# HGRN2 recurrence: the input gate's multiply moved into the exponents, and two VectorE steps reordered

## The chip, the cores and the metric

One core of one Trainium2 chip runs the whole program. The metric is the device time of one execution in microseconds.

## The reference, cut to what matters

The program is one inference step of a two-layer decoder trunk for a prompt of 512 tokens and 8 sample streams of 4 tokens each (544 columns in all), model width 1024, all in fp32. Layer 0 mixes with a gated convolution and windowed attention, layer 1 with an HGRN2 recurrence of 8 heads; each layer ends in a convolutional feed-forward part. The change is in layer 1's recurrence. Per head, with 128 key and 128 value channels:

```python
q, f, i, g = jnp.split(xn @ w_in, ...)
log_f = jnp.logaddexp(jnp.log(lb), jnp.log1p(-lb) + jax.nn.log_sigmoid(f))
k_in = (1.0 - lb) * jax.nn.sigmoid(-f)
# in chunks, with G the running sum of log_f inside a chunk:
decay = jnp.exp(jnp.where(causal, G_t - G_s, -jnp.inf))
A = einsum(q_t, k_s, decay)                       # scores inside the chunk
o = A @ v + (q * exp(G)) @ S
S = exp(G_last) * S + (k * exp(G_last - G)).T @ v
# then
o = rms_norm(o, norm_g) * silu(g);  out = o @ w_out
```

## The kernel before, in words

Every projection is a run of weight "units" (128 output channels). A unit is two halves of four 128-row weight tiles. ScalarE rounds each half to fp32r (`w_hi`, L844), VectorE takes the rest (`w_lo`, L1299), and TensorE makes three passes of 2 matmuls for each tile (`half`, L428): 24 matmuls a half. Halves follow each other all through the program. A weight half is split four halves ahead of its use.

The recurrence is written by hand between these halves. A head has 4 units (forget logit f, q, v, gate g), so 8 halves, and after each half every engine runs one "tick" (`hgrn_tick(t, prev, cur)`, t = 0 to 7): part of the current head `cur` and part of the one before, `prev`, whose outputs are still being finished. Each engine runs its own list strictly in order, and the engines meet at semaphores. Heads 1 to 7 have `prev`; head 0 has none, and only its last two units lie inside the ticks. After head 7, ticks 0 to 4 for `prev` = 7 run between the first halves of the output projection. In what follows head n is the stretch in which `cur` = n.

What the engines do in a head, as far as the change or the prediction's steps touch it:

- Tick 1. VectorE evacuates the forget logit (`head_out`, L1722) and clamps it (L1725). ScalarE makes exp(-f), ln(1 + .), exp(-.) = sigmoid(f) (L1198 to L1202), copies two score levels into `AT` (L1209, L1213) and rounds a weight half. TensorE multiplies score levels 1 and 2 (L704, L709).
- Tick 2. VectorE takes score levels (L1709), makes `kk` = the input gate k (L1782, one fused instruction on exp(-f), 1 - lb and sigmoid(f)) and the forget gate (L1783, L1785); ScalarE takes its logarithm (L1219); VectorE's scan gives `G` (L1790).
- Tick 3. VectorE evacuates q, splits a weight half, then runs `kd_and_diag`: `kd` = G_last - G (L1671, L1673 for the sample columns) and `E2` = G - G of the middle of each 8 columns (L1676, L1678). After that it adds the new sample state `Snew` (L1773, two instructions). TensorE runs the output matmuls (L748 to L762). ScalarE makes exp(kd), and GpSimd multiplies it by `kk` (L1950).
- Tick 4. TensorE waits for `Snew` (it needs the two PSUM banks) and for ScalarE's squares, then sums squares (L769, L770). VectorE scales the output gate (L1752, L1754) and makes the differences of levels 0 and 1 (`level_ops`, L1646, one 128x512 instruction a level). ScalarE makes `E1` = exp(diff) (L1236) and `E2` = exp(-diff) (L1237).
- Tick 5. VectorE evacuates v, splits a weight half, makes the head's output product (L1759), the level 2 difference, the transposed keys' rest (L1684), `y_lo` (L1764), the q half of level 0 (`level_q`, L1652), and `E2` times `kk` (L1803). ScalarE rounds `y_hi` (L1232). GpSimd makes `E1` times q (L1956), then `key_level` for level 0 (L1969), `qG` = exp(G) times q (L1963), then `key_level` for levels 1 to 3. TensorE transposes `kd` (L779; in head 0 at tick 6).
- Tick 6. TensorE transposes v (L786). VectorE makes the level 3 difference.
- Tick 7. ScalarE makes the level 3 exponentials (L1242, L1243), then scales the old sample states (L1251, eight instructions).
- Tick 0 of the next head. ScalarE rounds a weight half (L844) and starts the output gate. VectorE splits the half (L1299), takes the diagonal scores (L1709, L1739) and chains the states (L1657, L1660). TensorE multiplies the diagonal (L718 on `c_E`), and later, in tick 2, levels 3 and 4 (L718 on `lev`).

The lines that set who waits are these two of TensorE, with the order of VectorE in tick 3:

```python
if t == 4: pe.wait_ge(C["snew_ready"], 2 * prev + 2)
if t == 3: kd_and_diag(cur); dve.wait_ge(C["s0_scaled"], prev + 1); ... Snew += A[z]
```

## Time and profile before

| what | value |
|---|---|
| median of 3 runs | 1373.17 us (1372.12 to 1373.91) |
| the profiled execution's own time | 1372.79 us |
| its span, first to last instruction | 1371.0 us |
| mean granted TensorE clock | 0.992 |
| TensorE matmuls busy | 1331.7 us, 97% |
| VectorE busy | 820.6 us, 60% |
| ScalarE busy | 590.2 us, 43% |
| GpSimd busy | 249.5 us, 18% |
| recurrence with its ticks | 631 to 916 us of the span |
| one head of the steady part (761.08 to 795.20) | PE 33.01, DVE 28.11, ACT 22.66, POOL 9.53 us busy of 34.12 |

The span is what the trace covers; the time of the execution is 1.79 us longer, since it holds the start and the end around it. "Busy" counts an instruction from its start to its end, and an instruction that stands waiting for something inside itself counts as busy. The idle time in brackets at a row's end is the engine's pause before that row, with what ended it.

### The profile page before, as it was taken

Reading aid. Unit: us, or ns where it says so; the run is one execution under the profiler, and the core shown is the slowest. Engines: PE = TensorE matmul, PEld = TensorE weight load, DVE = VectorE, ACT = ScalarE, POOL = GpSimd, SP = SyncE. Lnnn points to the kernel's source line nnn. Section 1 sums busy time; section 2 is a strip of 40 time slices with the busy share of each in tenths; the row PEclk is TensorE's granted clock in tenths of the full one; section 3 lists DMA queues with packets and bytes.
Section 4 is the critical chain, followed back from the end, with each engine's and each line's share of the span. In section 5 each row is a group of like instructions: output and inputs, shape, how many; then the busy total and the mean of one; then the engine's idle time right before and its main releaser. Section 6 shows DMA issues by size and latency. Waiting matters only on the chain.

```text
span 1371.0 us, 30087 instructions
## 1 busy us (share of the span) xinstructions
PE 1331.7 (97%) x11724; PEld 1297.3 (95%) x11724; DVE 820.6 (60%) x1401; ACT 590.2 (43%) x1198; POOL 249.5 (18%) x373
## 2 busy tenths in 40 slices
PE   8999999999999999997999999989999999999997
PEld 8988999999999999996999999989999999999996
DVE  6467486656555632248788888867665555562224
ACT  5344354433333322236666666655533333332221
POOL 2123121111111101001222222212111111120000
PEclk9999999999999999999999999999999999999999
DMA  7411231222222322212222222323122232232211
GB/s 272 122 49 47 78 109 47 93 81 87 91 78 91 120 86 86 89 51 91 96 94 94 94 94 94 95 79 96 57 94 78 91 92 92 82 125 95 85 43 66
DMA packets 39682, 123.37 MB, mean 90 GB/s; under 512 B 4232, under 2 KB 12040, under 8 KB 39496
## 3 DMA queue, kind: packets, MB, share of 16 engines
q1 hardware_dynamic: 35400, 111.92, 25.1%
q10 hardware_dynamic: 4048, 10.20, 2.2%
q8 instruction: 41, 0.67, 0.2%
q0 software_dynamic: 176, 0.44, 0.1%
q14 instruction: 17, 0.14, 0.0%
HBM read 113.98 MB, written 8.57 MB: 89 GB/s over the span
## 4 chain that ended last, share of the span: by engine, by line
PE 77%; DVE 11%; ACT 6%; issue 5%; POOL 1%; DMA 0%; ACTq 0%; DVEq 0%; SPq 0%; POOLq 0%
PE acc L428 73%; DVE w_lo L1299 1%; ACT w_hi L844 1%; DVE lev L1646 1%; DVE x L1501 1%; ACT Snew L1251 1%; DVE Snew L1773 1%; DVE mix L1496 1%; DVE AT L1709 1%; PE aux L585 1%; DVE scratch L1759 1%; ACT AT L1213 0%; DVE h_lo L1308 0%; PE aux L597 0%; DVE lev L1652 0%
## 5 line engine op out<-in xcount | busy, mean ns | idle before, releaser
L1299 DVE TENSOR_TENSOR w_lo<-raw,w_hi 128x512 fp32r<-128x512 f32 (+1 forms) x372 | 316.3, 854 | 342.5 <-ACT w_hi L844 342.0
L428 PE MATMUL acc<-h_hi,w_hi 128*128 128x272 f32 x2208 | 478.7, 295 | 7.0 <-DVE h_lo L1308 2.4
L428 PE MATMUL acc<-h_hi,w_lo 128*128 128x272 f32 x2208 | 466.0, 289 | 0.0
L428 PE MATMUL acc<-h_lo,w_hi 128*128 128x272 f32 x2208 | 465.1, 289 | 0.0
L428 PEld LDWEIGHTS acc<-h_hi,w_hi 128*128 128x128 f32 x2208 | 351.6, 189 | 19.3 <-issue 8.0
L844 ACT CAST w_hi<-raw 128x512 fp32r<-128x512 f32 (+1 forms) x372 | 236.5, 642 | 288.2 <-PE acc L428 283.2
L428 PEld LDWEIGHTS acc<-h_lo,w_hi 128*128 128x128 f32 x2208 | 352.0, 190 | 0.2
L428 PEld LDWEIGHTS acc<-h_hi,w_lo 128*128 128x128 f32 x2208 | 349.6, 190 | 0.0
L428 PE MATMUL acc<-g_hi,w_hi 128*128 128x272 f32 x704 | 153.1, 288 | 0.0
L428 PE MATMUL acc<-g_hi,w_lo 128*128 128x272 f32 x704 | 153.0, 289 | 0.0
L428 PE MATMUL acc<-g_lo,w_hi 128*128 128x272 f32 x704 | 152.3, 288 | 0.0
L428 PEld LDWEIGHTS acc<-g_hi,w_hi 128*128 128x128 f32 x704 | 113.4, 188 | 0.1
L428 PEld LDWEIGHTS acc<-g_lo,w_hi 128*128 128x128 f32 x704 | 113.4, 189 | 0.1
L428 PEld LDWEIGHTS acc<-g_hi,w_lo 128*128 128x128 f32 x704 | 112.7, 189 | 0.0
L1924 POOL TENSOR_TENSOR scratch<-scratch,rstd 128x544 f32<-128x544 f32 x44 | 59.9, 1361 | 169.3 <-ACT scratch L1127 169.3
L1127 ACT ACTIVATE scratch<-scratch 128x544 f32<-128x544 f32 x44 | 29.0, 659 | 112.2 <-DVE scratch L1321 112.2
L1859 POOL TENSOR_TENSOR scratch<-scratch 128x272 f32<-128x272 f32 (+1 forms) x35 | 39.1, 1116 | 199.1 <-ACT scratch L994 151.3
L428 PE MATMUL acc<-y_hi,w_hi 128*128 128x272 f32 x256 | 69.6, 292 | 1.7 <-DVE y_lo L1764 1.6
L1133 ACT CAST g_hi<-scratch 128x544 f32 (+1 forms) x44 | 28.5, 647 | 98.1 <-DVE scratch L1605 93.6
L428 PE MATMUL acc<-y_hi,w_lo 128*128 128x272 f32 x256 | 68.8, 289 | 0.0
L428 PE MATMUL acc<-y_lo,w_hi 128*128 128x272 f32 x256 | 68.3, 287 | 0.0
L1123 ACT ACTIVATE scratch<-scratch,vec 128x544 f32<-128x544 f32 x44 | 33.0, 751 | 65.7 <-DVE scratch L1599 64.0
(247 smaller groups left out, 1424.4 us busy)
## 6 DMA issues: line engine op xcount, KB each, us to landing
raw<-in_w_up SPq DMA_DIRECT2D x88, 512.0 KB, 3.5
raw<-in_w_down SPq DMA_DIRECT2D x32, 704.0 KB, 4.1
raw<-in_w_in_c SPq DMA_DIRECT2D x32, 512.0 KB, 3.5
raw<-in_w_in_ab SPq DMA_DIRECT2D x18, 512.0 KB, 3.7
raw<-in_w_out_ab SPq DMA_DIRECT2D x8, 512.0 KB, 3.6
S<-in_state ACTq DMA_DIRECT2D x8, 512.0 KB, 3.6
o_ss<-Snew ACTq DMA_DIRECT2D x8, 512.0 KB, 2.7
raw<-in_w_out_c SPq DMA_DIRECT2D x8, 512.0 KB, 3.6
```

The costliest lines, as they stand in the source:

```text
L428: mm = pe.matmul(acc[out][:, t, 0:H], w[slot][:, wc], mv[:, kk_, t * H:(t + 1) * H], start=start and k == 0 and q == 0, stop=stop and k == ...
L585: mm = pe.matmul(A[g][:, j * 256 + lo_k:j * 256 + 256], q_sb[rows, 2 * pair + j, n * WIN:(n + 1) * WIN], k_sb[rows, (n - 1) * WIN + lo_k:( ...
L844: act.copy(w_hi[slot][:, to:to + kts * P], raw[n % 4][:, cols]).then_inc(hi_ready, 1)
L1123: act.activation(S[1][:], S[0][:], ACT.Copy, scale=vec[:, bass.ds(w + u + 2 * i, 1)]).then_inc(tap_ready, 1)
L1127: act.activation(S[2][:], S[1][:], ACT.Gelu_apprx_tanh).then_inc(act_done, 1)
L1133: act.copy(g_hi[:, u + 2 * i, :], S[3][:]).then_inc(g_hi_ready, 1)
L1251: i_ = act.activation(Snew[:, b, :], S0[:, b, :], ACT.Copy, scale=eG[:, last:last + 1])
L1299: dve.tensor_tensor(w_lo[slot][:, to], raw[n % 4][:, cols], w_hi[slot][:, to], ALU.subtract).then_inc(lo_ready, 1)
L1496: step.mark(dve.tensor_tensor(mix[:, k, cols(t)], mix[:, k, cols(t)], S[3][:, cols(t)], ALU.mult))
L1501: dve.scalar_tensor_tensor(x[:, k, cols(t)], mix[:, k, cols(t)], col(gain, k), x[:, k, cols(t)], ALU.mult, ALU.add).then_inc(x_new, 1)
L1859: pool.tensor_tensor(S[2][:, q], S[2][:, q], S[k % 2][:, q], ALU.add).then_inc(sq_added, 1)
L1924: pool.tensor_tensor(S[2][:], S[2][:], rstd[:], ALU.mult).then_inc(gate_ready, 1)
```

## The change

The key-side products of k with an exponential become sums before the exponential. Since k = (1 - lb) exp(-f) sigmoid(f), ln k = ln(1 - lb) - f + ln sigmoid(f). VectorE's fused instruction of tick 2 now makes -ln k in `S[0]` in place of `kk`, from the logit, ln(1 - lb) and ln(1 + exp(-f)). The buffer of `kk` is named `Gk`. It holds the sigmoid and the forget gate first, and after the scan `Gk` = G - ln k, a new 128x544 addition. The differences that need k use `Gk` where they used `G`. GpSimd's multiplies of `kd` and of the four levels are gone, VectorE's of `E2` too. `E1` needs a difference of its own, so the diagonal has four VectorE instructions in place of two, and a level's difference is two instructions of 128x256 in place of one of 128x512. `kd_and_diag` is cut in two; the diagonal's part stands behind the sample state. GpSimd starts on `E1` when ScalarE's first exponential of the pair is done. ln(1 - lb) is made once, after layer 0's mixer, by one VectorE and one ScalarE instruction of 8 columns. VectorE waits for GpSimd's `qG` of the head before it overwrites q.

```diff
@@ TensorE, hgrn_tick
-                        pe.wait_ge(C["diag_ready"], 2 * prev + 2)
+                        pe.wait_ge(C["diag_ready"], prev + 1)
+                        pe.wait_ge(C["diag_exp"], 2 * prev + 2)
...
-                        pe.wait_ge(C["lev_ready"], 8 * prev + 8)
+                        pe.wait_ge(C["lev_ready"], 4 * prev + 4)
@@ ScalarE, after_out and hgrn_tick
+                if post == 1:
+                    act.wait_ge(C["lb_ready"], 2)
+                    act.activation(lb[:, 4, :], lb[:, 3, :], ACT.Ln).then_inc(C["lb_done"], 1)
...
-                        step.mark(act.activation(S[0][:], S[0][:], ACT.Exp, scale=-1.0))
+                        step.mark(act.activation(S[1][:], S[0][:], ACT.Exp, scale=-1.0))
...
-                        act.activation(S[1][:], S[1][:], ACT.Exp, scale=-1.0).then_inc(C["sig_ready"], 1)
+                        act.activation(Gk[:], S[1][:], ACT.Exp, scale=-1.0).then_inc(C["sig_ready"], 1)
...
-                        act.activation(kd[:], kd[:], ACT.Exp).then_inc(C["kd_exp"], 1)
+                        act.activation(kd[:], kd[:], ACT.Exp).then_inc(C["kd_ready"], 1)
...
-                        act.activation(E1[:], E2[:], ACT.Exp)
+                        act.activation(E1[:], E1[:], ACT.Exp).then_inc(C["diag_exp"], 1)
                         act.activation(E2[:], E2[:], ACT.Exp, scale=-1.0).then_inc(C["diag_exp"], 1)
@@ VectorE, level_ops
-                dve.tensor_tensor(v, g, mid, ALU.subtract).then_inc(C["lev_diff"], 1)
+                dve.tensor_tensor(v[:, :, 0, :], gk[:, :, 0, :], mid, ALU.subtract)
+                dve.tensor_tensor(v[:, :, 1, :], g[:, :, 1, :], mid, ALU.subtract).then_inc(C["lev_diff"], 1)
@@ VectorE, kd_and_diag becomes kd_ops and diag_ops
+                step.mark(dve.tensor_tensor(Gk[:], G[:], S[0][:], ALU.add))
+                step.wait(dve)
...
+            def diag_ops(cur):
...
+                for to, of in ((E1, G), (E2, Gk)):
+                    dve.tensor_tensor(to[:, 0:TP].rearrange("p (c s) -> p c s", s=8),
+                                      of[:, 0:TP].rearrange("p (c s) -> p c s", s=8),
+                                      g8[:, :, 3:4].broadcast_to([P, TP // 8, 8]), ALU.subtract)
@@ VectorE, hgrn_tick and head_out
+                    if t == 3:
+                        dve.wait_ge(C["qG_ready"], cur)
...
-                        kd_and_diag(cur)
+                        kd_ops(cur)
                     dve.wait_ge(C["s0_scaled"], prev + 1)
...
+                    if cur is not None:
+                        diag_ops(cur)
...
-                    dve.scalar_tensor_tensor(kk[:], S[0][:], one_lb, S[1][:], ALU.mult, ALU.mult)
+                    dve.scalar_tensor_tensor(S[0][:], S[0][:], ln_one_lb, S[1][:], ALU.subtract, ALU.add)
...
-                    dve.wait_ge(C["diag_exp"], cur + 1)
-                    dve.tensor_tensor(E2[:], E2[:], kk[:], ALU.mult).then_inc(C["diag_ready"], 1)
@@ GpSimd, hgrn
-                    pool.wait_ge(C["kd_exp"], cur + 1)
-                    pool.tensor_tensor(kd[:], kd[:], kk[:], ALU.mult).then_inc(C["kd_ready"], 1)
...
-                    pool.wait_ge(C["diag_exp"], cur + 1)
+                    pool.wait_ge(C["diag_exp"], 2 * cur + 1)
                     pool.tensor_tensor(E1[:], E1[:], qn[:], ALU.mult).then_inc(C["diag_ready"], 1)
-                    for l in range(4):
-                        key_level(l, cur)
...
+                    pool.tensor_tensor(qG[:], eG[:], qn[:], ALU.mult).then_inc(C["qG_ready"], 1)
```

VectorE, the loop over heads 1 to 6, from the end of tick 3's weight split through tick 4 (`c_G`, `c_Gk`, `c_E`, `c_kd` are G, Gk, E1 or E2, kd), before:

```order
L1299 TENSOR_TENSOR w_lo<-raw,w_hi 128x512
L1671 TENSOR_TENSOR c_kd<-c_G 128x512
L1673 TENSOR_TENSOR c_kd<-c_G 128x32
L1676 TENSOR_TENSOR c_E<-c_G 128x512
L1678 TENSOR_TENSOR c_E<-c_G 128x32
...
L1773 TENSOR_TENSOR Snew<-Snew,aux 128x512
...
L1299 TENSOR_TENSOR w_lo<-raw,w_hi 128x512
L1752 SCALAR_TENSOR_TENSOR c_sg<-aux,vec,c_sg 128x512
L1754 SCALAR_TENSOR_TENSOR c_sg<-aux,vec,c_sg 128x32
L1646 TENSOR_TENSOR lev<-c_G 128x512 x2
L1722 TENSOR_TENSOR c_vv<-acc,rstd 128x544
```

and after the change:

```order
L1303 TENSOR_TENSOR w_lo<-raw,w_hi 128x512
L1676 TENSOR_TENSOR c_Gk<-c_G,scratch 128x544
...
L1680 TENSOR_TENSOR c_kd<-c_G,c_Gk 128x512
L1682 TENSOR_TENSOR c_kd<-c_G,c_Gk 128x32
...
L1791 TENSOR_TENSOR Snew<-Snew,aux 128x512
L1690 TENSOR_TENSOR c_E<-c_G 128x512
L1693 TENSOR_TENSOR c_E<-c_G 128x32
L1690 TENSOR_TENSOR c_E<-c_Gk,c_G 128x512
L1693 TENSOR_TENSOR c_E<-c_Gk,c_G 128x32
```

Ahead of the state stand three instructions in place of four; the diagonal's four stand behind it, ahead of the weight split, the gate and four half-width level differences, all before the evacuation of v.

GpSimd, the same loop, ticks 3 to 7, before:

```order
L1950 TENSOR_TENSOR c_kd<-c_kd,c_kk 128x544
...
L1956 TENSOR_TENSOR c_E<-c_E,c_qn 128x544
...
L1969 TENSOR_TENSOR lev<-lev,c_kk 128x4x64
L1963 TENSOR_TENSOR c_qG<-c_eG,c_qn 128x544
...
L1969 TENSOR_TENSOR lev<-lev,c_kk 128x8x32
```

and after:

```order
L1975 TENSOR_TENSOR c_E<-c_E,c_qn 128x544
...
L1979 TENSOR_TENSOR c_qG<-c_eG,c_qn 128x544
```

The two products with q now stand next to each other, and nothing of `kd` or the levels is left on this engine.

## Rows read from the trace of the kernel before

**Rows 1.** Waits of TensorE, whole span: engine, line waited for, us in total, times, longest.
```profile
PE aux L769 <- DVE Snew L1773: 6.2, 7, 1.0
```

**Rows 2.** Timeline of TensorE, heads 1, 4, 5 and 7: start us, us, engine line op.
```profile
664.02 0.45 PE L704 MATMUL aux<-lev 128*64 128x64 f32 x8
...
678.50 0.73 PE L769 MATMUL aux<-scratch,ones 128*128 128x272 f32 x2 [0.44 <-DVE Snew L1773]
...
765.56 0.45 PE L704 MATMUL aux<-lev 128*64 128x64 f32 x8
...
780.96 0.73 PE L769 MATMUL aux<-scratch,ones 128*128 128x272 f32 x2 [0.97 <-DVE Snew L1773]
...
815.10 0.73 PE L769 MATMUL aux<-scratch,ones 128*128 128x272 f32 x2 [0.95 <-DVE Snew L1773]
...
883.48 0.72 PE L769 MATMUL aux<-scratch,ones 128*128 128x272 f32 x2 [0.98 <-DVE Snew L1773]
```

**Rows 3.** Timeline of VectorE, forget-logit evacuation to new sample state, heads 1 and 4.
```profile
664.13 0.72 DVE L1722 TENSOR_TENSOR scratch<-acc,rstd 128x544 f32<-128x544 f32 x1 [0.53 <-PE acc L428]
...
766.59 0.72 DVE L1722 TENSOR_TENSOR scratch<-acc,rstd 128x544 f32<-128x544 f32 x1
...
778.21 0.69 DVE L1671 TENSOR_TENSOR c_kd<-c_G 128x512 f32<-128x512 f32 x1
...
779.62 1.28 DVE L1773 TENSOR_TENSOR Snew<-Snew,aux 128x512 f32<-128x512 f32 x2
```

**Rows 4.** Timeline of VectorE, head 4, ticks 5 to 7 and the next tick 0.
```profile
785.18 0.72 DVE L1722 TENSOR_TENSOR c_vv<-acc,rstd 128x544 f32<-128x544 f32 x1 [1.50 <-PE acc L428]
...
787.36 1.26 DVE L1759 TENSOR_TENSOR scratch<-scratch,c_sg 128x544 f32<-128x544 f32 x1
788.54 1.84 DVE L1646 TENSOR_TENSOR lev<-c_G 128x512 f32<-128x512 f32 x1
...
792.38 0.71 DVE L1803 TENSOR_TENSOR c_E<-c_E,c_kk 128x544 f32<-128x544 f32 x1
...
796.70 0.75 DVE L1652 TENSOR_TENSOR lev<-lev,c_qn 128x256 f32<-128x256 f32 x2
797.94 0.69 DVE L1299 TENSOR_TENSOR w_lo<-raw,w_hi 128x512 fp32r<-128x512 f32 x1 [0.49 <-ACT w_hi L844]
```

**Rows 5.** Timeline of GpSimd, head 4, ticks 4 and 5.
```profile
785.52 1.36 POOL L1956 TENSOR_TENSOR c_E<-c_E,c_qn 128x544 f32<-128x544 f32 x1 [4.41 <-ACT c_E L1237]
...
788.00 1.84 POOL L1963 TENSOR_TENSOR c_qG<-c_eG,c_qn 128x544 f32<-128x544 f32 x1
```

**Rows 6.** Timeline of ScalarE, head 4, tick 5 to the next tick 0.
```profile
788.74 0.65 ACT L1232 CAST y_hi<-scratch 128x544 f32 x1 [1.22 <-DVE scratch L1759]
...
794.33 0.42 ACT L1242 ACTIVATE lev<-lev 128x256 f32<-128x256 f32 x1 [1.24 <-DVE lev L1646]
...
797.30 0.60 ACT L844 CAST w_hi<-raw 128x512 fp32r<-128x512 f32 x1
```

**Rows 7.** Timelines of GpSimd, VectorE and TensorE, head 0, ticks 4 to 6.
```profile
646.90 1.37 POOL L1956 TENSOR_TENSOR c_E<-c_E,c_qn 128x544 f32<-128x544 f32 x1 [0.37 <-ACT c_E L1237]
...
645.66 1.42 DVE L1299 TENSOR_TENSOR w_lo<-raw,w_hi 128x512 fp32r<-128x512 f32 x1 [0.53 <-ACT w_hi L844]
647.00 2.42 DVE L1646 TENSOR_TENSOR lev<-c_G 128x512 f32<-128x512 f32 x2
...
646.59 1.11 PE L779 MATMUL aux<-ident,c_kd 128*128 128x128 f32 x4 [4.25 <-POOL c_kd L1950]
...
650.11 1.12 PE L786 MATMUL aux<-ident,c_vv 128*128 128x128 f32 x4 [2.20 <-DVE c_vv L1722]
```

**Rows 8.** Busy time by stretch: us, PE, PEld, DVE, ACT, POOL, PEclk, DMA, GB/s.
```profile
654.00:656.00 2.00, 2.00 (x10) 2.00 (x10) 2.00 (x4) 0.81 (x4) 0.79 (x1) 0.50 0.07 23
```

**Rows 9.** Timeline of TensorE, last head's output part.
```profile
895.48 0.43 PE L718 MATMUL aux<-c_E 128*32 128x32 f32 x29 [0.73 <-issue]
...
905.39 0.70 PE L748 MATMUL aux<-vbd,kt_s 96*128 96x512 f32 x2 [0.25 <-DVE AT L1709]
```

More of the change, by code:

```diff
@@ L236, in build @@
                 with ExitStack() as b:
-                    kk, G, qn, vv, gn, sg, eG, kd, qG, E1, E2 = [
+                    Gk, G, qn, vv, gn, sg, eG, kd, qG, E1, E2 = [
                         sb(f"c_{n}", [P, T], F32, b)
-                        for n in ("kk", "G", "qn", "vv", "gn", "sg", "eG", "kd", "qG", "E1", "E2")]
+                        for n in ("Gk", "G", "qn", "vv", "gn", "sg", "eG", "kd", "qG", "E1", "E2")]
                     lev = [sb(f"lev{i}", [P, TP], F32, b) for i in range(len(SPANS))]
@@ L1641, in level_ops @@
             def level_ops(l, cur):
[L1643 to L1646 removed]
+                v, g, gk = [z.rearrange("p (n a s) -> p n a s", a=2, s=SPANS[l]) for z in (lev[l][:], G[:, 0:TP], Gk[:, 0:TP])]
+                mid = g[:, :, 0, SPANS[l] - 1:SPANS[l]].broadcast_to([P, TP // (2 * SPANS[l]), SPANS[l]])
+                dve.tensor_tensor(v[:, :, 0, :], gk[:, :, 0, :], mid, ALU.subtract)
+                dve.tensor_tensor(v[:, :, 1, :], g[:, :, 1, :], mid, ALU.subtract).then_inc(C["lev_diff"], 1)
             def level_q(l, cur):
@@ L1665, in states, with kd_ops @@
                 i_.then_inc(C["st_ready"], 1)
-            def kd_and_diag(cur):
+            def kd_ops(cur):
                 dve.wait_ge(C["G_ready"], cur + 1)
-                gp, gs_ = G[:, 0:TP].rearrange("p (c s) -> p c s", c=NCH), sample(G[:, TP:T])
+                step.mark(dve.tensor_tensor(Gk[:], G[:], S[0][:], ALU.add))
+                step.wait(dve)
+                gp, gk = [z[:, 0:TP].rearrange("p (c s) -> p c s", c=NCH) for z in (G, Gk)]
+                gs_, gks = sample(G[:, TP:T]), sample(Gk[:, TP:T])
                 dve.tensor_tensor(kd[:, 0:TP].rearrange("p (c s) -> p c s", c=NCH),
-                                  gp[:, :, CH - 1:CH].broadcast_to([P, NCH, CH]), gp, ALU.subtract)
-                dve.tensor_tensor(sample(kd[:, TP:T]), gs_[:, :, TS - 1:TS].broadcast_to([P, NB, TS]), gs_,
+                                  gp[:, :, CH - 1:CH].broadcast_to([P, NCH, CH]), gk, ALU.subtract)
+                dve.tensor_tensor(sample(kd[:, TP:T]), gs_[:, :, TS - 1:TS].broadcast_to([P, NB, TS]), gks,
                                   ALU.subtract).then_inc(C["kd_diff"], 1)
+            def diag_ops(cur):
+                gs_ = sample(G[:, TP:T])
                 g8 = G[:, 0:TP].rearrange("p (c s) -> p c s", s=8)
-                dve.tensor_tensor(E2[:, 0:TP].rearrange("p (c s) -> p c s", s=8), g8,
-                                  g8[:, :, 3:4].broadcast_to([P, TP // 8, 8]), ALU.subtract)
-                dve.tensor_tensor(sample(E2[:, TP:T]), gs_, gs_[:, :, 1:2].broadcast_to([P, NB, TS]),
-                                  ALU.subtract).then_inc(C["diag_diff"], 1)
+                for to, of in ((E1, G), (E2, Gk)):
+                    dve.tensor_tensor(to[:, 0:TP].rearrange("p (c s) -> p c s", s=8),
+                                      of[:, 0:TP].rearrange("p (c s) -> p c s", s=8),
+                                      g8[:, :, 3:4].broadcast_to([P, TP // 8, 8]), ALU.subtract)
+                    i_ = dve.tensor_tensor(sample(to[:, TP:T]), sample(of[:, TP:T]),
+                                           gs_[:, :, 1:2].broadcast_to([P, NB, TS]), ALU.subtract)
+                i_.then_inc(C["diag_diff"], 1)
             def kdT_lo(cur):
@@ L1791, in hgrn_tick @@
                 if prev is None and t == 3:
-                    kd_and_diag(cur)
+                    kd_ops(cur)
+                    diag_ops(cur)
                 if t == 4:
@@ L1948, in hgrn @@
                 if cur is not None:
-                    pool.wait_ge(C["kd_exp"], cur + 1)
-                    pool.tensor_tensor(kd[:], kd[:], kk[:], ALU.mult).then_inc(C["kd_ready"], 1)
-                if cur is not None:
                     if prev is None:
@@ L1954, in hgrn @@
                     pool.wait_ge(evac, tile("in_c", 1) + 4 * cur)
-                    pool.wait_ge(C["diag_exp"], cur + 1)
+                    pool.wait_ge(C["diag_exp"], 2 * cur + 1)
                     pool.tensor_tensor(E1[:], E1[:], qn[:], ALU.mult).then_inc(C["diag_ready"], 1)
-                    for l in range(4):
-                        key_level(l, cur)
-                        if l == 0:
-                            if prev is not None:
-                                pool.wait_ge(C["oc_done"], prev + 1)
-                            pool.wait_ge(C["eG_ready"], cur + 1)
-                            pool.tensor_tensor(qG[:], eG[:], qn[:], ALU.mult).then_inc(C["qG_ready"], 1)
-            def key_level(l, cur):
-                pool.wait_ge(C["lev_exp"], 4 * cur + l + 1)
-                v, k_ = [z.rearrange("p (n a s) -> p n a s", a=2, s=SPANS[l]) for z in (lev[l][:], kk[:, 0:TP])]
-                pool.tensor_tensor(v[:, :, 0, :], v[:, :, 0, :], k_[:, :, 0, :], ALU.mult).then_inc(C["lev_ready"], 1)
+                    if prev is not None:
+                        pool.wait_ge(C["oc_done"], prev + 1)
+                    pool.wait_ge(C["eG_ready"], cur + 1)
+                    pool.tensor_tensor(qG[:], eG[:], qn[:], ALU.mult).then_inc(C["qG_ready"], 1)
             pool.wait_ge(half_done, 2 * UNIT0["in_c"])
```

19 lines of the change are left out of this document (10 added, 9 removed).

## The prediction

> **What bounds the kernel now.** I read the page first: TensorE's matmuls are busy for 97% of the span. So I read next what TensorE waits for. The longest sum is 6.2 us in 7 waits for the new sample state, one per head from 1 to 7 [rows 1]. The timeline shows them: 0.44 us in head 1, then 0.95 to 0.98 us [rows 2]. From head 1 to head 7 the six steps take 883.48 - 678.50 = 204.98 us, 34.16 each; from head 4 to head 5 it is 34.14. A wait of 0.97 us can be short because TensorE is slow to ask, or because the state is late, so I followed it back with the chain of waits. VectorE takes the forget logit at 766.59 and TensorE goes on at 780.96, 14.37 us later; in head 1 it is 678.50 - 664.13 = 14.37 as well [rows 2, 3]. That piece is a fixed run of VectorE and ScalarE work. The start differs. In head 1 VectorE stood ready (idle 0.53 until TensorE's half was done) and started 0.11 us after TensorE went to the level matmuls (664.02). In head 4 TensorE was there at 765.56 and VectorE came only at 766.59, 0.92 us later than those 0.11 us allow [rows 2, 3]. It was still busy with tick 0, which had begun with a wait of 0.49 us for a weight half of ScalarE at 797.94 (the same point one head on) [rows 4]. ScalarE was late because it had waited 1.24 us for the level 3 difference at 794.33, and started that half at 797.30 [rows 6]. VectorE made that difference late because its tick 5 is stretched: the output product takes 1.26 us and the level 2 difference 1.84 us, while GpSimd multiplies [rows 4, 5]. So the steady heads are bound by a **loop of VectorE and ScalarE**: state, tick 5, level 3, sample scaling, weight half, states, logit, state. TensorE keeps up with 0.97 us to spare. What shortens the stretched tick 5 is worth time, up to the point where VectorE is ready when TensorE's half ends.
>
> **Piece 1, logit to sample state.** The evacuation of q, the scan and the split stay. Ahead of the state, two diagonal differences leave and the addition G - ln k comes. The four differences take 779.62 - 778.21 = 1.41 us [rows 3], a pair 0.70. The new addition is 128x544 from two SBUF operands, like the product at 792.38, 0.71 us [rows 4]; with the wait for its own result 0.74. Net +0.04 us. The fused instruction of tick 2 keeps its form. Putting the state ahead of the diagonal thus only pays for the addition. Piece 1 becomes 14.41 us.
>
> **Piece 2, state to the next logit.** I lay the changed lists on the times of head 4; the state's adds end at 780.9 [rows 3]. Then the diagonal, now four instructions: 1.41, to 782.3. Weight split 0.61 and the gate's two steps 0.8: 783.75. The differences of levels 0 and 1 are now four of 128x256. Two such instructions took 0.75 us from the first's start to the last's end [rows 4], 0.34 each when they follow one another; so 1.36, to 785.1. The evacuation of v started at 785.18 after 1.50 us of idle time [rows 4]. The 1.4 us of diagonal and 0.15 us for the split differences fit into this idle time, with nothing left over.
>
> GpSimd starts its product with q when the first exponential is done, one ScalarE instruction of 544 columns earlier than 785.52: `y_hi` has that size and takes 0.65 us, of which some 0.55 count in a row of them, so about 785.0 [rows 5, 6]. It and VectorE then want the same thing. When GpSimd's `qG` started at 788.00 VectorE's product of 1.26 us was still running to 788.62, and VectorE's level 2 difference started at 788.54 and ended at 790.38, 0.54 us after `qG` ended at 789.84 [rows 4, 5]. Undisturbed it is 0.68 us. This is what taking turns looks like, a whole instruction each, not a slowdown of both by a share. The **Trainium skill**, "SBUF — State Buffer", on who interferes with whom, states it as a rule: a VectorE instruction with two SBUF inputs and a GpSimd instruction hold a shared port pair in turn, and the loser blocks fully. The trace agrees in every such pair that I looked at; it matters most in head 0, below, where turns and shares give sums of their own.
>
> Taking turns: GpSimd's product runs 785.1 to 786.4, and `qG` follows at once to 787.7. VectorE's split, due at 786.53, waits for it and ends at 788.3; the output product runs free to 789.0, 0.4 us later than before. ScalarE's `y_hi` moves from 788.74 to 789.1. From there GpSimd is silent. Before, ScalarE took 797.30 - 788.74 = 8.56 us to its weight half, 1.24 of it waiting for level 3 [rows 6]. Now VectorE has level 3 at about 792.2 (level 2 0.68, the keys' rest 0.28, `y_lo` 0.65, level 0's q half 0.34, a split 0.6, level 3 0.68), ahead of ScalarE's need at 793.4 (794.33 - 1.24, shifted by 0.35): the product of 0.71 with `kk` is gone, and GpSimd's level products no longer stand between. So ScalarE's half starts at 789.1 + 7.32 = 796.4 rather than 797.30. VectorE's split starts at 797.0 rather than 797.94, and it is ready for the logit 2.80 us later (800.73, one head after 766.59, less 797.94), at 799.8. TensorE's half allows it at 765.56 + 34.14 + 0.11 = 799.81. They meet.
>
> So the logit starts 18.85 us after L769 (780.96), plus 14.41, gives a head of 33.26 us against 34.14. As the two arrive together I take 0.85 us of the 0.88. **Six steps, heads 2 to 7: -5.1 us.** In head 1 the logit was already on time: +0.04. Bounds: nothing gained if the stretch isn't what holds the loop; at the other end TensorE has no wait left in these steps, 0.97 and the 0.37 us by which its way from L704 to the end of tick 4's half is longer in head 4 than in head 1 ((780.96 - 0.97 - 765.56) - (678.50 - 0.44 - 664.02) = 0.39), 8 us in six.
>
> **Head 0.** TensorE waits 4.25 us for `kd`, which GpSimd multiplies last, and 2.20 us for v [rows 7]. `kd` now comes from ScalarE about 0.7 us earlier, worth nothing: v comes last. Ahead of v stood two level differences, 2.42 us with GpSimd's product of 1.37 us in them [rows 7]. Now VectorE has the addition (0.74) and four diagonal steps for two (+0.7), while the split, which took 1.42 us beside GpSimd's `kd` against 0.69 alone, goes free [rows 4, 7]; the differences start at about 647.1 as before, four of them. GpSimd asks at 647.4. In turns: one and a half differences, GpSimd's product to 649.1, one difference, `qG` to 650.75, the last one: v starts at 651.05, 1.7 us later. If both engines only slowed each other it would be 0.4 us later. Without a second hold, it is 0.35 us. The clock pays part back. TensorE, idle before, was granted 0.50 (1.2 GHz) up to 656, six us after it took up work at 650.11 [rows 7, 8]. If the clock comes back at the same moment, the later start saves half of 1.7 at the half clock, and 0.85 is left; if it comes later too, 1.7. I take **+1.3 us**; ends -0.7 (only `kd` counted) and +1.7.
>
> **Last head.** TensorE waits 0.73 us at 895.48 for VectorE's product of `E2` with `kk` [rows 9], which is gone. Then it waits for the diagonal scores and the states, and VectorE is held in `vbd` by GpSimd's gate product; TensorE starts the sample matmuls at 905.39, after another 0.25 us for the scores [rows 9]. VectorE is 1.55 us ahead by piece 2's working plus the wait for a split that no longer holds it; `vbd` then gets its turn before GpSimd asks. I get 903.65 for L748. **-1.7 us**; ends -0.7 and -2.2. Nothing after it changes.
>
> **The lower bound's logarithm** adds one instruction of 8 columns to VectorE and ScalarE in a stretch in which the chain runs through TensorE's matmuls alone: 0. GpSimd's lost work counts only through the turns. The new wait for `qG` of the head before has long been met: `qG` ends at 789.84 and the wait stands a head later. No DMA is moved.
>
> **Sum:** -5.1 + 0.04 + 1.3 - 1.7 = -5.5 us against the profiled execution's 1372.79, 1367.3. The median of the runs is 0.38 us above it, so 1367.7.
>
> **Rivals.**
> - *GpSimd gets its turn before the last level difference* (B). It asks at 785.0, the last difference starts at 784.8; 0.2 us decide. Then v and the split come 0.3 us later, a head gains 0.55: -3.3 in place of -5.1, so 1369.5. Chance 0.2.
> - *GpSimd and VectorE don't block each other a second time in head 0, and TensorE's chain in the heads is freed fully* (C): head 0 +0.35, heads -5.3, last -2.2: 1366.0. For it: the stretch of rows 4 has room. Against: the turns in rows 4 and 5. Chance 0.13.
> - *The loop is held elsewhere* (D), say by the evacuation of v, which now meets a VectorE without idle time. Then the heads give 0 to -1.5, and head 0 and the last nearly cancel: 1371.3 to 1372.8. Against it: 1.24 us of ScalarE's wait come from the stretch. Chance 0.15.
> - *Slower* (E): a half-width difference with its broadcast operand costs as much as a full one, 0.60 in place of 0.34. Then levels 0 and 1 end 1.04 us later, v and the split behind both GpSimd products, the output product ends at 790.1, level 3 is late again, and a head takes 0.2 us more than before: +1.2, head 0 +2.6, last head 0: 1377.0. It decides from about 0.55 us a difference. Against it: the strided q halves of the same size at 0.34 [rows 4]. Chance 0.07.
>
> The main case (A) has 0.45. Faster by more than 0.2% (2.7 us, about what a measurement of this kernel can tell from no change): A, B, C, 0.78, and a bit of D, 0.01. Within 0.2%: D, 0.14. Slower: E, 0.07. Range: from C's lower side, 1364.8, to 1371.3, which takes in A, B and the lower edge of D; E and most of D, 0.19, lie outside.
>
> **What would show it.** L769's wait in heads 2 to 7 falls to about 0.4 us (as in head 1) and L748 no longer waits for the scores; heads are 33.3 us apart; ScalarE's wait for level 3 is gone; VectorE's split of tick 5 takes about 1.8 us beside `qG`; in head 0 L786 starts near 651.8. I am wrong if L769 still waits 0.9 us, if half-width differences take over 0.5 us, or if heads stay 34.1 apart.

## The result and the profile after

The changed kernel takes 1364.57 us (median of 4 runs, 1362.98 to 1364.97) against 1373.54 us before (4 runs), a ratio of 0.9936 with a 95% interval of 0.9924 to 0.9948: 9.0 us faster. The prediction said faster, 1367.7, with a range from 1364.8, and the result lies 0.2 us below that range; the forecast gain of 5.5 us is 61% of the measured one. The profiled execution took 1364.97 us.

The page's second line, the kernel after (busy time, share of the span and instructions of each engine):

```profile
PE 1329.5 (98%) x11724; PEld 1296.3 (95%) x11724; DVE 813.9 (60%) x1450; ACT 589.7 (43%) x1199; POOL 206.8 (15%) x333
```

TensorE does the same work; VectorE has 49 instructions more and is busy 6.7 us less, GpSimd 42.7 us less. The waits of TensorE (us in total, times, longest), where [rows 1] had 6.2 us in 7 waits:

```profile
PE aux L770 <- DVE Snew L1791: 3.7, 7, 0.6
```

The timeline of TensorE in heads 1, 4, 5 and 7, the answer to [rows 2]:

```profile
663.30 0.45 PE L704 MATMUL aux<-lev 128*64 128x64 f32 x8
...
677.84 0.73 PE L770 MATMUL aux<-scratch,ones 128*128 128x272 f32 x2 [0.52 <-DVE Snew L1791]
...
777.77 0.73 PE L770 MATMUL aux<-scratch,ones 128*128 128x272 f32 x2 [0.51 <-DVE Snew L1791]
...
811.08 0.73 PE L770 MATMUL aux<-scratch,ones 128*128 128x272 f32 x2 [0.50 <-DVE Snew L1791]
...
877.76 0.72 PE L770 MATMUL aux<-scratch,ones 128*128 128x272 f32 x2 [0.61 <-DVE Snew L1791]
```

Heads 4 and 5 are 811.08 - 777.77 = 33.31 us apart (34.14 before), and the six steps from head 1 to head 7 take 199.92 us in place of 204.98. VectorE in head 4, tick 5 to the next head's logit, the answer to [rows 3, 4]:

```profile
781.46 0.42 DVE L1652 TENSOR_TENSOR lev<-c_G 128x256 f32<-128x256 f32 x1
782.01 0.72 DVE L1740 TENSOR_TENSOR c_vv<-acc,rstd 128x544 f32<-128x544 f32 x1
783.35 1.61 DVE L1303 TENSOR_TENSOR w_lo<-raw,w_hi 128x512 fp32r<-128x512 f32 x1 [0.61 <-ACT w_hi L845]
784.88 0.71 DVE L1777 TENSOR_TENSOR scratch<-scratch,c_sg 128x544 f32<-128x544 f32 x1
785.52 0.41 DVE L1651 TENSOR_TENSOR lev<-c_Gk,c_G 128x256 f32<-128x256 f32 x1
...
793.58 0.69 DVE L1303 TENSOR_TENSOR w_lo<-raw,w_hi 128x512 fp32r<-128x512 f32 x1 [1.21 <-ACT w_hi L845]
...
796.65 0.72 DVE L1740 TENSOR_TENSOR scratch<-acc,rstd 128x544 f32<-128x544 f32 x1 [0.19 <-PE acc L428]
```

GpSimd's two products with q, the answer to [rows 5]:

```profile
781.72 1.38 POOL L1975 TENSOR_TENSOR c_E<-c_E,c_qn 128x544 f32<-128x544 f32 x1 [18.10 <-ACT c_E L1240]
783.06 1.35 POOL L1979 TENSOR_TENSOR c_qG<-c_eG,c_qn 128x544 f32<-128x544 f32 x1
```

and ScalarE, the answer to [rows 6]:

```profile
785.72 0.65 ACT L1236 CAST y_hi<-scratch 128x544 f32 x1 [1.39 <-DVE scratch L1777]
...
789.98 0.41 ACT L1246 ACTIVATE lev<-lev 128x256 f32<-128x256 f32 x1
...
792.95 0.60 ACT L845 CAST w_hi<-raw 128x512 fp32r<-128x512 f32 x1
```

The loop has opened where the prediction said. GpSimd's products stand end to end (781.72, 783.06), VectorE's weight split waits for the second (1.61 us), and after 784.40 nothing holds VectorE: the output product takes 0.71 us (1.26 before), a level's half 0.41. ScalarE no longer waits for level 3 (no idle time before 789.98), and its weight half starts 15.18 us after the squares' sum at 777.77, against 797.30 - 780.96 = 16.34 before. At 796.65 VectorE stands ready for the logit and waits 0.19 us for TensorE, as it did only in head 1 before.

Head 0 went otherwise than forecast. GpSimd, VectorE and TensorE there, the answer to [rows 7]:

```profile
648.74 2.28 POOL L1975 TENSOR_TENSOR c_E<-c_E,c_qn 128x544 f32<-128x544 f32 x1 [34.36 <-ACT c_E L1240]
650.99 1.79 POOL L1979 TENSOR_TENSOR c_qG<-c_eG,c_qn 128x544 f32<-128x544 f32 x1
...
648.40 0.42 DVE L1651 TENSOR_TENSOR lev<-c_Gk,c_G 128x256 f32<-128x256 f32 x1
648.74 0.42 DVE L1652 TENSOR_TENSOR lev<-c_G 128x256 f32<-128x256 f32 x1
649.07 0.42 DVE L1651 TENSOR_TENSOR lev<-c_Gk,c_G 128x256 f32<-128x256 f32 x1
649.41 0.42 DVE L1652 TENSOR_TENSOR lev<-c_G 128x256 f32<-128x256 f32 x1
649.74 0.72 DVE L1740 TENSOR_TENSOR c_vv<-acc,rstd 128x544 f32<-128x544 f32 x1
650.45 1.12 DVE L1303 TENSOR_TENSOR w_lo<-raw,w_hi 128x512 fp32r<-128x512 f32 x1
651.50 1.56 DVE L1651 TENSOR_TENSOR lev<-c_Gk,c_G 128x256 f32<-128x256 f32 x1
...
647.22 1.11 PE L780 MATMUL aux<-ident,c_kd 128*128 128x128 f32 x4 [3.59 <-ACT c_kd L1228]
...
650.52 1.11 PE L787 MATMUL aux<-ident,c_vv 128*128 128x128 f32 x4 [1.97 <-DVE c_vv L1740]
```

and the busy time by stretch with the granted clock (the value behind the busy times of PE, PEld, DVE, ACT and POOL), the answer to [rows 8]:

```profile
652.00:654.00 2.00, 2.00 (x11) 2.00 (x10) 1.94 (x4) 1.14 (x4) 0.78 (x1) 0.52 0.58 123
654.00:656.00 2.00, 2.00 (x18) 2.00 (x17) 1.97 (x6) 1.65 (x7) 0.00 (x0) 1.00 0.37 147
```

The last head's output part, the answer to [rows 9]:

```profile
888.96 0.46 PE L718 MATMUL aux<-c_E 128*32 128x32 f32 x32
...
897.62 0.70 PE L749 MATMUL aux<-vbd,kt_s 96*128 96x512 f32 x2
```

Where the 9 us came from, measured between marks that both traces have (the scan of head 0 starts at 641.85 before and at 643.14 after; the changed kernel's profiled execution is 1.3 us late by then, and its mean granted clock is the lower one already in the first 100 us, in layer 0 and ahead of anything that was changed, 0.95 against 0.97, so the recurrence is compared from its own start):

| stretch | before | after | difference | forecast |
|---|---|---|---|---|
| head 0: scan to first level matmul (L704) | 22.17 | 20.16 | -2.01 | +1.3 |
| head 1: L704 to the squares' sum | 14.48 | 14.54 | +0.06 | +0.04 |
| six steps, squares' sum of head 1 to head 7 | 204.98 | 199.92 | -5.06 | -5.1 |
| last head's sum to the matmul after `y_lo` | 33.12 | 31.06 | -2.06 | -1.7 |
| sum | 274.75 | 265.68 | -9.07 | -5.5 |

The two sums are 3.6 us apart, and 3.3 us of that is head 0.

### The profile page after: what moved, and what is told of

Read it like the earlier page. It is cut to its first block, busy times and chain, and to the rows that moved or that the text cites. A ratio compares the mean times of both kernels' runs of the same rounds, so it can differ in the third digit from the quotient of the medians.

```text
span 1363.2 us, 30063 instructions
## 1 busy us (share of the span) xinstructions
PE 1329.5 (98%) x11724; PEld 1296.3 (95%) x11724; DVE 813.9 (60%) x1450; ACT 589.7 (43%) x1199; POOL 206.8 (15%) x333
## 4 chain that ended last, share of the span: by engine, by line
PE 83%; DVE 7%; ACT 4%; issue 4%; POOL 1%; DMA 0%; DVEq 0%; SPq 0%; ACTq 0%; POOLq 0%
PE acc L428 78%; DVE w_lo L1303 1%; DVE x L1507 1%; PE aux L733 1%; DVE Snew L1791 1%; DVE mix L1502 1%; ACT w_hi L845 1%; PE aux L585 1%; DVE h_lo L1312 0%; PE aux L597 0%; ACT AT L1217 0%; PE aux L770 0%; ACT scratch L1223 0%; ACT scratch L1202 0%; PE aux L508 0%
## 5 line engine op out<-in xcount | busy, mean ns | idle before, releaser
L1303 DVE TENSOR_TENSOR w_lo<-raw,w_hi 128x512 fp32r<-128x512 f32 (+1 forms) x372 | 319.7, 863 | 345.9 <-ACT w_hi L845 345.2
```

Of the source, the lines that this page charges most:

```text
L1303: dve.tensor_tensor(w_lo[slot][:, to], raw[n % 4][:, cols], w_hi[slot][:, to], ALU.subtract).then_inc(lo_ready, 1)
```

## The experiments

Each kernel was run with the kernel before beside it, and ratios are to that one. Three were run once, for the trace: the wide differences, the waits between them, and the one without the `kd` product.

### The order alone

The kernel before, with the diagonal's differences moved behind the sample state:

```diff
-    (in kd_and_diag)  E2 = G - mid      # two instructions
     Snew += A[z]
+    E2 = G - mid
```

> The kernel before, with the diagonal's two differences moved behind the new sample state and nothing else. Loop theory: the piece from the forget logit to the state loses 0.70 us (14.37 to 13.67) and the 0.7 us fit into VectorE's 1.50 us of idle time ahead of v, so steady heads go from 34.14 to about 33.45 us apart, six steps give -4.1 us, head 1's wait of 0.44 goes, head 0 unchanged; in all 4 to 5 us faster, ratio near 0.997. Rival (tick 5's stretch alone counts, the state's place does not): heads stay at 34.1, ratio 1.000.

Measured: 1366.92 us against 1372.53, ratio 0.9953 (0.9938 to 0.9968): 5.6 us faster, somewhat more than the 4 to 5 expected. In the trace, the stretches of the table above give 5.0 us. Head 1's wait is gone. TensorE in heads 4 and 5:

```profile
779.22 0.73 PE L769 MATMUL aux<-scratch,ones 128*128 128x272 f32 x2 [0.27 <-DVE Snew L1777]
...
812.66 0.73 PE L769 MATMUL aux<-scratch,ones 128*128 128x272 f32 x2 [0.28 <-DVE Snew L1777]
```

33.44 us apart, with a wait of 0.27 us; the loop theory had said 33.45. The rival that the state's place does not count falls. The order alone gives as much as the level products gone alone (below).

### The order undone

The changed kernel with `diag_ops` ahead of the state again.

```diff
     kd_ops(cur)
+    diag_ops(cur)
     Snew += A[z]
-    diag_ops(cur)
```

> The changed kernel with its four diagonal differences put back ahead of the new sample state. Loop theory: TensorE's wait at the squares' sum (0.51 us in a head) grows by 1.41 to about 1.9 us, since VectorE meets TensorE's half at the logit in any case; heads 34.7 us apart in place of 33.31, some 1.4 x 7 = 9.8 us slower than the changed kernel, so about 1 us slower than the kernel before, ratio 1.001. Rival (the removed multiplies carry the gain, the order nothing): ratio stays at 0.994.

Measured: 1375.95 us, ratio 1.0025 (1.0016 to 1.0035): slower than before, with all five of GpSimd's multiplies by the input gate gone. TensorE in heads 2, 3 and 4:

```profile
714.58 0.72 PE L770 MATMUL aux<-scratch,ones 128*128 128x272 f32 x2 [1.92 <-DVE Snew L1792]
...
750.79 0.73 PE L770 MATMUL aux<-scratch,ones 128*128 128x272 f32 x2 [1.92 <-DVE Snew L1792]
...
785.50 0.73 PE L770 MATMUL aux<-scratch,ones 128*128 128x272 f32 x2 [1.90 <-DVE Snew L1792]
```

The wait is 1.90 to 1.92 us, 1.4 longer, as expected. Heads 3 and 4 are 34.71 apart; heads 2 and 3 are 36.21. The page by stretch (same columns) shows why in head 2:

```profile
714.00:720.00 6.00, 5.42 (x27) 5.27 (x28) 3.28 (x8) 3.35 (x7) 1.47 (x2) 0.72 0.26 100
720.00:726.00 6.00, 6.00 (x52) 5.98 (x51) 5.56 (x12) 5.01 (x14) 1.22 (x1) 1.00 0.28 87
```

After a pause of 1.92 us the granted clock averages 0.72 in these six microseconds, so TensorE went at 1.2 GHz for somewhat over half of them, and is at 1.00 in the next. Two of the six steps show it, 1.5 us each; the other four, after the same pause, don't. In this execution the stretches of the table take 278.03 us, 3.3 more than before, and 3.0 of these are the two falls. The median is 3.4 us above the kernel before, where 1 us had been expected. How many falls the other nine executions had isn't shown; their times run from 1374.19 to 1379.71 us.

### GpSimd's level products gone, order as before

The kernel before, `key_level` left out on GpSimd; the input gate is missing from the four off-diagonal levels. As in the changed kernel, VectorE waits for `qG` of the head before it overwrites q.

```diff
-                    for l in range(4):
-                        key_level(l, cur)
```

> The kernel before without GpSimd's products of the four levels with the input gate (so the gate is missing from the four off-diagonal levels of the scores); order and all else as before, with the wait for qG ahead of the evacuation of q. Loop theory: tick 5 shrinks, VectorE is ready for the logit before TensorE's half is done, heads 34.14 - 0.88 = 33.26 to 33.3 us apart, squares' wait 0.44 us in each head, six steps -5.2 us. Rival (the state's order carries the gain): heads stay at 34.1 us and ScalarE still waits for level 3. Head 0: the two level differences no longer meet a level product before v, but GpSimd's product with q as before, so L786 starts near 650.1 as before, relative to the same start.

Measured: 1366.67 us, ratio 0.9953 (0.9937 to 0.9968). The squares' sums of heads 4 and 5 are at 778.70 and 812.13, 33.43 us apart; their wait is 0.66 us, not 0.44. The reason is in the same turns: GpSimd's two products with q run end to end, VectorE's output product takes 1.88 us beside the second of them, and VectorE is ready for the logit only at 797.76, 0.2 us after TensorE (L704 at 797.46). So tick 5 alone gives 0.7 us a head, and each of the two edits alone reaches about 33.44. Head 0 missed the expectation: v was transposed 9.41 us after the scan's start in place of 8.26, 1.15 us later than before. GpSimd, then VectorE:

```profile
646.61 1.37 POOL L1958 TENSOR_TENSOR c_E<-c_E,c_qn 128x544 f32<-128x544 f32 x1 [0.37 <-ACT c_E L1237]
647.95 1.78 POOL L1962 TENSOR_TENSOR c_qG<-c_eG,c_qn 128x544 f32<-128x544 f32 x1
...
646.72 3.56 DVE L1646 TENSOR_TENSOR lev<-c_G 128x512 f32<-128x512 f32 x2
```

Both level differences together take 3.56 us. GpSimd was first (646.61); difference, `qG`, difference follow in turns, with no semaphore wait between the two differences. This is just what the prediction had expected of the change.

### Wide differences

The changed kernel with a level's difference as one 128x512 instruction from G; the input gate is missing from the four levels.

```diff
-                dve.tensor_tensor(v[:, :, 0, :], gk[:, :, 0, :], mid, ALU.subtract)
-                dve.tensor_tensor(v[:, :, 1, :], g[:, :, 1, :], mid, ALU.subtract)
+                dve.tensor_tensor(v, g, mid, ALU.subtract)
```

> The changed kernel with each level's difference as one 128x512 instruction from G alone, as before the change (so the input gate is missing from the four levels). It asks why GpSimd did not get its turn in head 0 while four half-width differences ran. Theory 'short': instructions of 0.34 us follow each other too closely for GpSimd to get in; with 0.60 us instructions it gets in between level 0 and level 1 as the prediction had it, its product starts right after level 0's difference and v starts about 1.3 us late. Theory 'queued': a run of VectorE instructions without semaphore waits is passed on ahead and keeps the port to its end; then both wide differences run in 0.6 us each, v starts 0.15 us earlier than in the changed kernel, and GpSimd's product is longer than 2 us or starts with v.

GpSimd, then VectorE, in head 0:

```profile
647.34 2.15 POOL L1975 TENSOR_TENSOR c_E<-c_E,c_qn 128x544 f32<-128x544 f32 x1 [34.34 <-ACT c_E L1240]
...
646.99 1.29 DVE L1652 TENSOR_TENSOR lev<-c_G 128x512 f32<-128x512 f32 x2
```

"Short" falls: two 0.6 us instructions run undisturbed (1.29 us for both) and GpSimd's product, which started while the first ran, takes 2.15 us in place of 1.33. The single time is 1364.53 us. The heads are 33.28 us apart against 33.31, so the second instruction of each level is as good as free.

### Waits between the differences

```diff
+                if l == 1:
+                    dve.wait_ge(C["lev_diff"], 4 * cur + 1)
-                dve.tensor_tensor(v[:, :, 0, :], gk[:, :, 0, :], mid, ALU.subtract)
+                step.mark(dve.tensor_tensor(v[:, :, 0, :], gk[:, :, 0, :], mid, ALU.subtract))
+                step.wait(dve)
```

> The changed kernel with a semaphore wait for its own predecessor ahead of each half-width level difference. Theory 'queued': the run without waits is broken, GpSimd gets its turn between two differences in head 0, one difference takes about 1.6 us, v starts 1.3 to 2.6 us later than in the changed kernel. Theory 'short': the differences are as short as before, GpSimd still waits for all four, and v starts only some 0.2 us later (four waits).

GpSimd, then VectorE, in head 0:

```profile
648.65 1.33 POOL L1978 TENSOR_TENSOR c_E<-c_E,c_qn 128x544 f32<-128x544 f32 x1 [34.35 <-ACT c_E L1240]
649.94 1.52 POOL L1982 TENSOR_TENSOR c_qG<-c_eG,c_qn 128x544 f32<-128x544 f32 x1
...
648.31 0.42 DVE L1653 TENSOR_TENSOR lev<-c_Gk,c_G 128x256 f32<-128x256 f32 x1
648.77 1.50 DVE L1655 TENSOR_TENSOR lev<-c_G 128x256 f32<-128x256 f32 x1
650.30 1.44 DVE L1653 TENSOR_TENSOR lev<-c_Gk,c_G 128x256 f32<-128x256 f32 x1
651.78 0.42 DVE L1655 TENSOR_TENSOR lev<-c_G 128x256 f32<-128x256 f32 x1
```

With a wait ahead of each, the same four instructions lose the port twice: the second takes 1.50 us and the third 1.44, and GpSimd's product runs in 1.33. v was transposed 9.84 us after the scan's start, against 7.38 in the changed kernel, 2.46 later. "Queued" had said 1.3 to 2.6. Its single time is 1367.80 us.

### GpSimd's `kd` product gone, order as before

```diff
-                    pool.wait_ge(C["kd_exp"], cur + 1)
-                    pool.tensor_tensor(kd[:], kd[:], kk[:], ALU.mult).then_inc(C["kd_ready"], 1)
```

> The kernel before without GpSimd's product of kd with the input gate (so the gate is missing from the keys that go into the states). Theory of turns: in head 0 the weight split that took 1.42 us takes 0.7, so v comes 0.7 us earlier unless GpSimd's product with q starts correspondingly earlier against the differences; kd comes 1.4 us earlier than before. In heads 1 to 7 nothing changes, 34.14 us apart, as kd lies in the slack of tick 4. Rival: tick 4's GpSimd work holds the loop too, and heads come 0.2 us closer or more.

Heads stay 34.08 us apart with a wait of 0.97, against 34.14 before, so tick 4's product was worth 0.06 us a head and didn't hold the loop. The single time is 1369.06 us. In head 0, GpSimd, then VectorE:

```profile
646.50 1.86 POOL L1953 TENSOR_TENSOR c_E<-c_E,c_qn 128x544 f32<-128x544 f32 x1 [33.82 <-ACT c_E L1237]
...
645.86 1.29 DVE L1646 TENSOR_TENSOR lev<-c_G 128x512 f32<-128x512 f32 x2
```

VectorE was first by 0.64 us, both differences ran undisturbed (1.29 us), and GpSimd's product took 1.86 us. Since a difference takes 0.60 us in a row, the second had begun when GpSimd's product started: this run doesn't show whether GpSimd would have been passed over. v came 1.86 us earlier than before, not 0.7: 0.73 from the split and 1.13 from the differences.

### The last work ahead of the state moved too

The changed kernel with `kd_ops` behind the state.

```diff
-                    if cur is not None:
-                        kd_ops(cur)
                     dve.wait_ge(C["s0_scaled"], prev + 1)
...
+                        kd_ops(cur)
                         diag_ops(cur)
```

> The changed kernel with G - ln k and kd's differences behind the new sample state too, so nothing of the current head stands ahead of it. Loop theory: the piece to the state shrinks by 1.46 us, more than TensorE's remaining wait of 0.51, so that wait goes to 0 in all 7 heads, heads 32.8 us apart, 3.5 us faster than the changed kernel: ratio near 0.991. Rival (ScalarE, which now waits longer for kd, comes late to the weight half and the root of tick 4 and gives it back as a wait of TensorE for a weight half or for kd): ratio 0.994 or more.

Measured: 1362.91 us, ratio 0.9925 (0.9912 to 0.9939). TensorE in heads 4 and 5:

```profile
775.40 0.62 PE L770 MATMUL aux<-scratch,ones 128*128 128x272 f32 x2
...
802.12 0.70 PE L749 MATMUL aux<-vbd,kt_s 96*128 96x512 f32 x2 [0.22 <-issue]
```

The squares' wait is gone in all 7 heads. Heads 4 and 5 are 33.02 us apart (775.40 to 808.42), not 32.8: the sample matmuls (L749) wait 0.22 us. The profile names no releaser; that it is the scores that VectorE takes in tick 2 is my reading. The six steps take 197.77 us, 2.15 less than in the changed kernel, and the median is 1.7 us lower: half of the 3.5 that were expected. Head 1 gives 0.63 us more, and the last head takes 1.04 us back: TensorE waits 1.14 us there (887.38) for ScalarE's rounded v of the sample streams. The loop theory was right about the wait of the squares, and had put the rest too low.

### Head 0's v earlier

```diff
                     kd_ops(cur)
+                    head_out(5, cur)
                     diag_ops(cur)
```

> The changed kernel with head 0's evacuation of v moved from behind the level differences to between kd and the diagonal. Theory: v then is ready when TensorE has transposed kd, the wait of 1.97 us at L787 goes, and head 0 ends 2 us earlier, more if the granted clock returns earlier for it: 2 to 3 us faster than the changed kernel, ratio near 0.992. Rival (clock): after the shorter pause TensorE runs at the half clock for longer, and half of it or more is given back: less than 1 us faster.

Measured: 1363.06 us, ratio 0.9927 (0.9913 to 0.9940). TensorE in heads 0 and 1:

```profile
646.89 1.06 PE L787 MATMUL aux<-ident,c_vv 128*128 128x128 f32 x4
...
660.41 0.45 PE L704 MATMUL aux<-lev 128*64 128x64 f32 x8 [1.22 <-DVE AT_s L1757]
...
676.03 0.73 PE L770 MATMUL aux<-scratch,ones 128*128 128x272 f32 x2 [1.02 <-DVE Snew L1791]
```

v no longer waits. But TensorE then stands 1.22 us at the first level matmul, for the diagonal scores that VectorE takes, and 1.02 us at the squares' sum of head 1 in place of 0.52. From the scan to the first level matmul it is 18.72 us in place of 20.16, to the squares' sum 34.34 in place of 34.70: between these two traces 0.4 us are left of the 2 to 3 expected; the medians are 1.5 us apart. Neither theory had the two waits; what came next in head 0 was VectorE's own list, not the clock, as the granted clocks below show.

### Both, and `kd` first in head 0

The first kernel has the edits of the last two sections together:

> Both edits: kd behind the state, and head 0's v evacuated between kd and the diagonal. If the two gains are of different places they add: heads 33.0 us apart without a wait at the squares' sum, v ready when kd is transposed, from the first scan to the first level matmul 18.7 us, ratio to the kernel before about 0.991 (-12 us). Also, the 1.02 us wait of head 1 at the squares' sum is covered by the 1.46 us shorter piece. Rival: in head 1 TensorE stands waiting for the scores and states that VectorE takes late (1.2 us at the first level matmul), and some of the gain stays lost: 0.992.

Measured: 1362.99 us, ratio 0.9927 (0.9913 to 0.9940), where 0.991 had been expected if the two gains add and 0.992 if not: they don't add. From the scan to the first level matmul it is 18.72 us, as expected, but TensorE's wait there is 0.27 us, head 1 takes 14.47 us to the squares' sum in place of 13.91 with `kd` behind the state alone, and the six steps take 198.61 us in place of 197.77.

The second has these and, in head 0, VectorE's weight split of the norm's output behind v:

```diff
+                    split(2 * UNIT0["in_c"] + 7, 0)
                     diag_ops(cur)
```

> As the run with both edits, and in head 0 the weight split of tick 3 stands behind kd and v. Theory: kd is ready 0.6 us earlier (TensorE's wait of 3.59 us for it falls to 3.0), v still in time; 0.6 us faster than both edits alone, a difference below what the timed runs can tell, but visible in the trace: first kd transpose 3.5 us after the scan in place of 4.08. Rival: the half split later holds TensorE's half 7 and gives it back.

Measured: 1362.94 us, ratio 0.9924 (0.9910 to 0.9937). The scan to the matmul after `y_lo` is 263.94 and 264.05 us in the kernel with both edits and in this one, 265.12 with `kd` behind the state alone, 265.68 in the changed kernel, 274.75 before. The last edit brought `kd` 0.46 us forward (3.62 us after the scan in place of 4.08, where 3.5 had been expected), and gave it back, as its rival had said, though at other places: TensorE waits 1.31 us for the rounded values of the sample streams and 1.23 us for the diagonal scores before head 1. The busy time by stretch of this last kernel in head 0 (the value behind the five engines is the granted clock):

```profile
644.00:652.00 8.00, 7.33 (x58) 7.08 (x58) 7.37 (x14) 5.71 (x13) 4.07 (x2) 1.00 0.32 78
```

In this execution the granted clock didn't fall in head 0, and the first level matmul still starts 18.87 us after the scan. With v alone earlier the full clock was back 7.0 us after the scan's start, with both edits 9.6 us after it, and it is 18.72 us in both. Once v is early, the clock doesn't set when head 1 begins.

The four kernels lie within 0.2 us of each other by their medians, and 1.5 to 1.7 below the changed kernel; their intervals overlap with its own, so which of them is best stays open.

## Why the prediction was right and where it was wrong

**What bounds the kernel: right.** The loop of VectorE and ScalarE was named, and both of its halves were tested apart: 33.44 us with the state's order alone, 33.43 with the level products gone alone, 33.31 with both and the new work. The cover that the change used up, VectorE's 1.50 us ahead of v, was enough: v's evacuation starts 4.24 us after the squares' sum, against 4.22 before.

**Piece 1: right.** From the logit to the squares' sum it takes 811.08 - 796.65 = 14.43 us; 14.41 had been worked out, with +0.04 for the addition in place of a pair of differences.

**Piece 2: right, in all its steps.** Counted from the squares' sum: `y_hi` of ScalarE 8.1 us forecast, 7.95 measured; its weight half 15.4 and 15.18; VectorE's split 16.0 and 15.81; the logit 18.85 and 18.88; the head 33.26 and 33.31. The six steps gave -5.06 us where -5.1 had been put. The split that waits for `qG` took 1.61 us, where about 1.8 had been named as the sign. The wait at the squares' sum is 0.50 to 0.61 us in these heads, where about 0.4 had been named. For TensorE's longer way to the squares' sum in head 4 the prediction writes 0.37 us beside a bracket that gives 0.39; its bound of 8 us stays.

**Head 0: wrong, the step "In turns: one and a half differences, GpSimd's product to 649.1, one difference, `qG` to 650.75, the last one".** GpSimd asked as expected, after VectorE had begun its run, but did not get the turn: all four differences ran in 0.34 us each, and GpSimd's product took 2.28 us. v's matmul starts 7.38 us after the scan in place of 8.26, a gain of 0.88 us where a loss of 1.7 had been laid down before the clock: 2.6 of head 0's 3.3 us. The starting order was right; wrong was that GpSimd gets in at the next border between two of VectorE's instructions.

The runs show the conditions in part. Four differences in the changed kernel, and two wide ones, were not broken where VectorE had found nothing of GpSimd in its way when it began them. A semaphore wait inside the same run breaks it (1.50 and 1.44 us). But a run without waits can be broken too. In the same head 0, `qG` (650.99) gets in between the weight split (650.45) and the next level difference (651.50, 1.56 us), and before the change `qG` (788.00) gets in between the output product (787.36) and the level 2 difference (788.54) [rows 4, 5]; no wait stands between either pair. In these cases, and where two differences took 3.56 us with the level products gone, the VectorE instruction ahead had itself been held up by GpSimd (1.12 us for a split of 0.69, 1.26 for a product of 0.71). Whether that is the condition, or that GpSimd had just been running, stays open.

The bound of -0.7 us that the prediction gave as head 0's best end had counted only `kd`; it had no case in which nothing holds VectorE ahead of v.

**The clock in head 0: mis-sized, and a chance part.** The prediction took 0.4 us back from the clock (1.3 from 1.7). From v's matmul to the first level matmul it is 13.91 us before and 12.78 after, -1.13 us: the other 0.7 of head 0's 3.3 us. In this trace the granted clock goes back to 1.00 at 653.9 (v's matmul at 650.52); before, it did so at 656.0 (v's matmul at 650.11). The change cannot be credited with it: the kernel with `kd` behind the state has the same head 0 and needs 13.97 us, the one with the order undone 12.50, and the one with wide differences 13.80. So -0.9 us of the -2.0 are the change's, and about -1.1 are where the clock happened to rise in this execution. How much of it an average execution has was not measured.

**Last head: mis-sized.** The mechanism was right: the diagonal's 0.73 us wait is gone, and the sample matmuls start 19.86 us after the last squares' sum in place of 21.91. The term was -1.7 us and measures -2.06, since TensorE waits nowhere between the squares' sum at 877.76 and the sample matmuls, where before it waited 0.73, 0.67, 0.54 and 0.25 us, 2.19 in all. Which of these made the term larger than the 1.7 worked out wasn't taken apart.

**The rivals.** C, "don't block each other a second time in head 0", at 1366.0, was nearest, and still short: it had counted one hold of VectorE ahead of v (+0.35 us in head 0), and the trace shows none. E falls: a half-width difference costs 0.34 us. D falls with the six steps. B's 0.2 us margin held: GpSimd asked at 781.72, and the last difference had started at 781.46. Nor need it have decided: in the last head of the kernel with `kd` behind the state GpSimd's product started at 879.38, ahead of the last difference (879.49), and waited for it (1.76 us in place of 1.33).

## What to carry to other kernels

When TensorE's wait is short and the same in every round, follow it back until it closes on itself: a loop of two slower engines can be opened at its place of contention or by moving work behind the result that is waited for, and the two add only until the slower loop meets the busiest engine: one edit alone gave 0.7 us a head and the other 0.7, both together 0.83. Of the 0.51 us of wait then left, another 0.3 came off by moving `kd` behind the state too. Here putting work behind the state earned as much as removing four multiplies a head; removing all five, with the order undone and the new additions in, was slower than before. On a port that two engines share, look at which engine's work starts first, whether a semaphore wait stands inside its run, and whether the run's first instruction was itself held up, not only at how much each has to do.

## What the runs showed of the hardware

- VectorE instructions with two SBUF operands and GpSimd's multiplies held each other up for whole instructions (1.50 us for 0.42, 1.88 for 0.71). Where VectorE had begun a run of them unhindered and no semaphore wait stood inside it, GpSimd did not get in until its end (four of 0.34 us, two of 0.60 us). With a wait ahead of each it got in twice. Where the first had itself been held up, GpSimd got in behind it without a wait (split 1.12 us, difference 1.56 us). The Trainium skill, "SBUF — State Buffer", "SBUF: two separate sides", gives the pair of ports to whichever starts first, for the whole instruction; the trace agrees for one instruction (a split of 0.69 us takes 1.61 beside `qG`), and shows that it can go on for a run. That VectorE's later instructions are already asking when the first runs is a reading, not shown, and by itself it doesn't explain the runs that were broken without a wait.
- A pause of TensorE of 1.92 us was followed by six microseconds at a mean granted clock of 0.72 in one head, and such a fall came in two of the six steps and not in the other four of the same execution, whose pauses were as long. In head 0 a pause of 3.15 us was followed by no fall in one execution of the last kernel. The same code after v's matmul in head 0 took 12.50, 12.78 and 13.97 us in three kernels, by when the clock came back.
